# A two-layer hybrid transformer block on one core: the squares of the Strassen feed-forward moved to ScalarE, GpSimd's block sums held back, and the ends of that layer rearranged

## The chip, the core and the metric

The kernel runs on one core of a Trainium2 chip. Five engines work side by side and meet only through semaphores: TensorE (matmuls; PE in the profile), VectorE (DVE), ScalarE (ACT), GpSimd (POOL) and SyncE (SP), whose queue issues the loads. The metric is the device time of one execution in microseconds, lower is better.

## The reference, cut to what matters

```python
for layer in range(2):                       # x: 512 tokens, ctx: 256 tokens, width 1024
    ...                                      # norm, w_in, four mixers, w_out, x and ctx added to
    x = x + mod_l[5] * squared_relu_mlp(modulate(x, norm2_g[layer], mod_l[3], mod_l[4]),
                                        w_ff1[layer], w_ff2[layer])
    if need_ctx:                             # in layer 0 only
        ctx = ctx + ...                      # the same with mod_c
def squared_relu_mlp(h, w1, w2): return jnp.square(jax.nn.relu(h @ w1)) @ w2     # 1024 -> 4096 -> 1024
def rmsnorm(x, g): return x * lax.rsqrt(jnp.mean(x * x, -1) + EPS) * g
```

All of it is in float32. The kernel gets this precision from three passes per product: each operand is split into a rounded part ("hi", a copy on ScalarE) and what is left of it ("lo", a subtraction on VectorE or GpSimd), and TensorE adds up hi x hi, hi x lo and lo x hi.

## The kernel before

Activations lie transposed: `xT` holds 8 blocks of 128 features by T = 768 tokens (512 of x, 256 of ctx). No scheduler is involved. Each engine's program is written out by hand, and an engine works strictly in its written order; semaphores (`wait_ge`, `then_inc`) make it wait for the others. Weights come in units of 1 MB. `raw` has two slots, so SP issues the load of a unit as soon as the unit two places before it has been lowered (its lo part made) on GpSimd. The order of the units in layer 0's feed-forward is, for each chunk q: ff1 (q,0), ff1 (q,1), st (q,0), st (q,1).

**The feed-forward of layer 0** has 8 chunks (q = 0 to 7) of 512 hidden columns.

- ff1: two units j = 0, 1 of 256 columns. TensorE computes four groups each, (ct, s) = (0,0), (0,1), (1,0), (1,1): column half ct, and 512 (s = 0) or 256 (s = 1) tokens. The groups alternate between two PSUM banks (`gp`), and a bank is free again once ScalarE's `relu` has read it into `nsq`.
- The hidden values are squared (VectorE, in place) and turned into seven Strassen operands, in the order B11, T1, B21, T2, T3, T4, B22. T1 to T4 are sums (`h_sum`); each operand is copied by ScalarE (`h_high`) and subtracted by VectorE (`h_low`). A relu may overwrite `nsq` only when the operands that read it are lowered: that of (0,0) waits for T3's subtraction of the unit before.
- ff2: a Strassen product with 7 steps (`strassen`), in one unit per half of the output, st (q,0) and st (q,1); chunk 7 has only the first, and two ordinary units ff2 (7,2), ff2 (7,3) in place of the second. The weight blocks need four sums (`st_sum` n = 0 to 3) before they are copied (`block_high`, `fb_hi`, ScalarE) and subtracted (`fb_lo`, GpSimd, in `st_lower`). VectorE does these sums for st (q,0), GpSimd those for st (q,1). Sum n may be made only after GpSimd's subtraction n - 1; block copy 2 needs sum 1, copies 3 to 6 need sum 3.
- `st_add_back` on VectorE adds the steps' results to `xT`; step 2 needs the PSUM bank that step 0's add-back frees.

**The end of that layer.** `norm` of layer 1 needs the mean of squares: ScalarE squares the 8 blocks of `xT` (into `nsq`, two buffers), VectorE adds them up (`accumulate`, semaphore acc1), TensorE averages over the features, ScalarE takes logarithm and exponential, VectorE refines (L2225 to L2227) and scales (L2258), ScalarE makes `xhi` and VectorE `xlo`. The 256 ctx tokens go first, then the 512 of x; TensorE starts layer 1's first projection behind them. `after_unit` on ScalarE makes the hi part of the next weights.

## Time and profile before

| | us |
|---|---|
| median of 3 runs (2216.3 to 2225.04) | 2221.67 |
| the profiled execution | 2221.8 |
| its span | 2220.0 |
| busy in the span: TensorE, VectorE, ScalarE, GpSimd | 2027.1, 1226.8, 816.2, 806.2 |
| mean granted clock of TensorE | 0.958 |

The profile is one execution. Each row of a timeline has a start, the time it lasted, the engine, the line, what is written and read and how often; in brackets stands how long the engine had been idle and what it had waited for. A row with x4 is four instructions merged, its time that of all four. TensorE is the busiest engine by far, so the places where it stands still are the ones to read.

### The profile page before, as it was taken

The page shows a single profiled execution, that of the slowest core. Times are in us where ns is not written, and L with a number is a line of the kernel's source. Part 1 is how long each engine was busy: PE and PEld are TensorE (multiplying, and loading weights), DVE is VectorE, ACT ScalarE, POOL GpSimd, SP SyncE. Part 2 cuts the span into 40 slices and gives each one's busy share as a digit, 9 for nine tenths or more (in the row PEclk, how much of TensorE's full clock was granted, in tenths as well). Part 3 has the DMA queues.
Part 4 walks back from the last instruction along what each step waited for, and adds up shares of the span by engine and source line. Part 5 has one row for each costly group of instructions (what it writes and reads, how often), then busy time and mean ns, then how long its engine had stood idle before and what let it go on. Part 6 is the DMA issues. An engine that isn't in the chain of part 4 may idle for free.

```text
span 2220.0 us, 32559 instructions
## 1 busy us (share of the span) xinstructions
PE 2027.1 (91%) x13084; PEld 1720.0 (77%) x13084; DVE 1226.8 (55%) x2129; ACT 816.2 (37%) x1402; POOL 806.2 (36%) x641
## 2 busy tenths in 40 slices
PE   4899898989989799999999988998999888999998
PEld 3778786777877689889999867777787677778777
DVE  3555547846875666666666654545857765121122
ACT  2333324544454423333333333323554454232231
POOL 1231203012842255555565313213024523444452
PEclk8899998999999899999999999999999989999999
DMA  7320010452521121122211122010243312322322
GB/s 261 80 67 20 22 37 20 134 127 70 164 85 49 39 76 58 41 74 77 76 60 65 50 54 70 20 39 25 91 122 104 106 58 76 95 95 92 98 79 74
DMA packets 170694, 169.12 MB, mean 76 GB/s; under 512 B 29408, under 2 KB 159536, under 8 KB 170416
## 3 DMA queue, kind: packets, MB, share of 16 engines
q1 hardware_dynamic: 169744, 163.89, 24.2%
q10 hardware_dynamic: 800, 3.15, 0.4%
q8 instruction: 105, 1.72, 0.3%
q14 instruction: 45, 0.37, 0.1%
HBM read 159.15 MB, written 2.10 MB: 73 GB/s over the span
## 4 chain that ended last, share of the span: by engine, by line
PE 74%; DVE 13%; ACT 4%; issue 3%; DMA 2%; POOL 2%; SPq 2%; DVEq 0%; ACTq 0%; POOLq 0%
PE gp L1028 42%; PE sp L1287 3%; PE sp L1438 3%; PE gp L1324 2%; PE sp L1126 2%; PE gp L1082 2%; PE sp L1127 2%; PE sp L1128 2%; PE tp L1304 2%; SPq L833 1%; PE sp L1278 1%; PE gp L1052 1%; PE op L1304 1%; DVE small L2556 1%; DMA raw<-in_w_mod 1%
## 5 line engine op out<-in xcount | busy, mean ns | idle before, releaser
L917 POOL TENSOR_TENSOR wlo<-raw,whi 128x512 fp32r<-128x512 f32 x326 | 442.8, 1390 | 1029.4 <-ACT whi L1616 1029.2
L1028 PE MATMUL gp<-xhi,whi 128*128 128x512 f32 (+1 forms) x1416 | 517.4, 365 | 47.5 <-DVE xlo L2250 23.8
L1028 PE MATMUL gp<-xhi,wlo 128*128 128x512 f32 (+1 forms) x1416 | 503.8, 356 | 0.0
L1028 PE MATMUL gp<-xlo,whi 128*128 128x512 f32 (+1 forms) x1408 | 502.9, 357 | 0.0
L1028 PEld LDWEIGHTS gp<-xhi,whi 128*128 128x128 f32 x1416 | 275.4, 195 | 94.7 <-issue 23.2
L1028 PEld LDWEIGHTS gp<-xhi,wlo 128*128 128x128 f32 x1416 | 274.6, 194 | 39.3
L1028 PEld LDWEIGHTS gp<-xlo,whi 128*128 128x128 f32 x1408 | 273.7, 194 | 38.2 <-issue 1.8
L1616 ACT ACTIVATE whi<-raw 128x2048 fp32r<-128x2048 f32 (+2 forms) x86 | 159.0, 1849 | 205.1 <-PE gp L1028 129.5
L929 POOL TENSOR_TENSOR fb_lo<-raw,fb_hi 128x512 fp32r<-128x512 f32 x105 | 145.4, 1406 | 97.2 <-ACT fb_hi L1709 97.2
L2870 DVE SCALAR_TENSOR_TENSOR xT<-gp,mods,xT 128x512 f32<-128x512 f32 (+1 forms) x78 | 52.5, 680 | 172.2 <-PE gp L1028 160.3
L2556 DVE TENSOR_REDUCE small<-sp 128x1 f32<-128x768 f32 (+4 forms) x120 | 90.0, 792 | 51.3 <-PE sp L1287 51.3
L1028 PE MATMUL gp<-hhi,whi 128*128 128x512 f32 (+1 forms) x280 | 109.4, 391 | 3.5 <-issue 2.9
L1028 PE MATMUL gp<-hhi,wlo 128*128 128x512 f32 (+1 forms) x280 | 108.7, 388 | 0.0
L1028 PE MATMUL gp<-hlo,whi 128*128 128x512 f32 (+1 forms) x280 | 108.7, 388 | 0.0
L1709 ACT ACTIVATE fb_hi<-raw 128x512 fp32r<-128x512 f32 x105 | 59.6, 622 | 128.3 <-DVE raw L760 49.7
L2333 DVE SCALAR_TENSOR_TENSOR xT<-sp,mods,xT 128x128 f32<-128x128 f32 (+1 forms) x200 | 86.9, 490 | 33.0 <-PE sp L1128 32.7
L1126 PE MATMUL sp<-hhi,fb_hi 128*128 128x384 f32 x280 | 94.1, 336 | 6.3 <-DVE xT L2333 5.2
L2353 DVE TENSOR_TENSOR nsq<-nsq 128x512 f32<-128x512 f32 (+1 forms) x64 | 58.7, 920 | 65.5 <-ACT nsq L1686 65.3
L1127 PE MATMUL sp<-hlo,fb_hi 128*128 128x384 f32 x280 | 93.6, 334 | 0.0
L1128 PE MATMUL sp<-hhi,fb_lo 128*128 128x384 f32 x280 | 93.6, 334 | 0.0
L2302 DVE TENSOR_TENSOR hlo<-nsq,hhi 128x384 fp32r<-128x384 f32 (+1 forms) x112 | 77.5, 709 | 29.0 <-ACT hhi L1698 29.0
L1698 ACT ACTIVATE hhi<-nsq 128x384 fp32r<-128x384 f32 (+1 forms) x112 | 56.7, 528 | 92.4 <-DVE nsq L2317 53.4
(432 smaller groups left out, 4178.8 us busy)
## 6 DMA issues: line engine op xcount, KB each, us to landing
raw<-in_w_ff SPq DMA_DIRECT2D x63, 1024.0 KB, 5.4
raw<-in_w_mod SPq DMA_DIRECT2D x48, 1024.0 KB, 5.2
raw<-in_w_in SPq DMA_DIRECT2D x20, 1024.0 KB, 5.3
raw<-in_w_in SPq DMA_DIRECT2D x24, 256.0 KB, 4.6
bias<-e SPq DMA_DIRECT2D x96, 32.0 KB
raw<-in_w_out SPq DMA_DIRECT2D x12, 256.0 KB, 2.9
xin<-in_x ACTq DMA_DIRECT2D x1, 2048.0 KB, 9.7
raw<-in_w_out SPq DMA_DIRECT2D x16, 128.0 KB, 3.4
```

The source lines that it names most:

```text
L917: nc.gpsimd.tensor_tensor(wlo[:, s % 2, ks, :], raw[:, index[splits[s]] % 2, ks, :], whi[:, s % 2, ks, :].bitcast(F32), ALU.subtract)\
L929: nc.gpsimd.tensor_tensor(fb_lo[:, b, :, :, :], st_block(u, *ST_SOURCE[b]), fb_hi[:, b, :, :, :].bitcast(F32), ALU.subtract)\
L1028: mm = pe.matmul(out, lhs, rhs, start=(i == 0 and j == 0), stop=(i == end - 1 and j == 2))
L1126: pe.matmul(out, wh, high, start=(ST_OPENS[step] and m == 0), stop=False, skip_group_check=True)
L1127: pe.matmul(out, wh, low, start=False, stop=False, skip_group_check=True)
L1128: mm = pe.matmul(out, wl, high, start=False, stop=(m == 1), skip_group_check=True)
L1287: mm = pe.matmul(region(m, n, j, o, o + w), ql if i == 2 else qh, kl if i == 1 else kh, start=(i == 0 and not added), stop=(i == 2))
L1304: mm = pe.transpose((tp, op_)[half][:, P * (k - k0):P * (k - k0) + P], probs(m, n, j)[:, P * k:P * k + P], ident)
L1616: nc.scalar.activation(whi[:, s % 2, 0:k_tiles(v), :], raw[:, index[v] % 2, 0:k_tiles(v), :], ACT.Copy)\
L2302: V.tensor_tensor(low, src, high.bitcast(F32), ALU.subtract)\
L2333: ins = V.scalar_tensor_tensor(out=xT[:, k, a:b], in0=st_bank(u, step, pair)[:, a - lo:b - lo], scalar=mods[:, l, 40 + k, col:col + 1], in ...
L2556: V.tensor_reduce(small[:, c + j:c + j + 1], scored(m, n, j, w), AX.X, ALU.max, negate=True)\
```

## The change

Six edits, all around the feed-forward of layer 0 (lines by the diff):

1. The square of the hidden values is made by ScalarE right behind its relu, not by VectorE.
2. In chunk 0 the copies and sums of the first weight blocks come later: VectorE's sums 0 to 2 and ScalarE's block copies 0 to 2 behind the whole half j = 0, sum 3 and copies 3 to 6 into half j = 1.
3. In half j = 1 T4's sum moves behind the add-back of step 0.
4. GpSimd starts its sums for st (q,1) only when VectorE has added back step 0 of st (q,0).
5. For chunk 1 GpSimd lowers st (0,1) ahead of the weights of ff1 (1,0); ScalarE's copy of these weights moves behind the copies of st (0,1).
6. At the end, the last squares get two more buffers (`nsq2`, in the place of hidden blocks that are no longer read), `prepare` moves back, the weight copy moves behind the squares, and the two last add-backs and squares move into the first half of the normalisation.

```diff
+        nsq2, _ = place("nsq2", [P, 2, T], F32, scratch0 + 4 * T * 4)
+        last_square = lambda i: (nsq[:, 0, :], nsq[:, 1, :], nsq2[:, 0, :], nsq2[:, 1, :], nsq[:, 1, :], nsq2[:, 0, :])[i]
...
@@ st_lower (GpSimd)
+                if u[3]:
+                    pool.wait_ge(st_out, 2 * ST_STEPS * st_no["st", u[1], u[2], 0] + 2)
...
+                    if u in [("ff1", l, 1, 0) for l in ST_LAYERS]:
+                        st_lower(("st", u[1], 0, 1))
                     low(s)
...
-                    if j == 0 and q:
+                    if j == 0 and q > 1:
                         st_lower(("st", l, q - 1, 1))
@@ relu (ScalarE)
                 nc.scalar.activation(dst, bank(n)[:, 0:b - a], ACT.Relu).then_inc(bank_free[group_bank[n]], 1)
+                if l in ST_LAYERS:
+                    wait_read(act, None, n)
+                    nc.scalar.activation(dst, dst, ACT.Square).then_inc(ls(l, "h_sq"), 1)
@@ feed_forward_st (ScalarE)
-                            if j == 0 and (q == 0 or ct == 0):
-                                for b in range(3) if q == ct == 0 else range(3, ST_STEPS):
+                            if q == 0 and (j, ct) in ((0, 1), (1, 0)):
+                                for b in range(3) if j == 0 else range(3, ST_STEPS):
+                                    block_high(("st", l, 0, 0), b)
+                            if q and j == ct == 0:
+                                for b in range(3, ST_STEPS):
                                     block_high(("st", l, q, 0), b)
-                            if j == 1 and ct == (1 if q == 0 else 0):
+                            if q and j == 1 and ct == 0:
                                 after_unit(("ff1", l, q, 0))
...
-                    for i, k in enumerate((1, 3, 0, 2)):
...
                     u = ("ff2", l, ST_CHUNKS - 1, 2)
+                    for i, k in enumerate((1, 3, 0, 2, 4, 5)):
+                        if i < 4:
+                            act.wait_ge(st_out, 2 * ST_STEPS * st_no["st", l, ST_CHUNKS - 1, 0] + 11 + i)
+                        else:
+                            act.wait_ge(*upto(l + 1, "acc1", i - 3))
+                            for s in range(2):
+                                wait_read(act, None, N(u, (k % 2, s)))
+                        nc.scalar.activation(last_square(i), xT[:, k, :], ACT.Square).then_inc(ls(l + 1, "sq1"), 1)
                     after_unit(u)
-                    squares(l + 1, 1, 2, u)
                     u = ("ff2", l, ST_CHUNKS - 1, 3)
                     closing_squares(l + 1, 1, u, 0)
-                    norm(l + 1, 1, lambda: closing_squares(l + 1, 1, u, 1))
+                    norm(l + 1, 1, lambda: closing_squares(l + 1, 1, u, 1, done=True),
+                         {5: lambda: closing_square(l + 1, 1, u, 1, 0), 7: lambda: closing_square(l + 1, 1, u, 1, 1)})
@@ feed_forward_st (VectorE)
-                                a, b = SEGS[c[1]]
-                                wait_read(dve, None, N(u, c))
-                                V.tensor_tensor(nsq[:, ct, a:b], nsq[:, ct, a:b], nsq[:, ct, a:b], ALU.mult).then_inc(ls(l, "h_sq"), 1)
...
-                                if j == 0:
-                                    for n in range(3) if q == 0 else (3,):
-                                        st_sum(dve, V, first, n)
+                                if j == (0 if q else 1):
+                                    st_sum(dve, V, first, 3)
                                 continue
-                            for name in ("T2", "T3", "T4"):
-                                h_sum(l, q, j, name)
+                            h_sum(l, q, j, "T2")
+                            h_sum(l, q, j, "T3")
+                            if j == 0:
+                                h_sum(l, q, j, "T4")
...
                             st_add_back(first, 0)
+                            h_sum(l, q, j, "T4")
                             h_low(l, q, j, "T3")
...
-                    norm(l + 1, 1, closing=lambda: add_back(u, 5, l, cs=cs[2:]))
+                    prepare(l + 1)
+                    norm(l + 1, 1, inside={4: lambda: add_back(u, 5, l, cs=cs[2:3]), 6: lambda: add_back(u, 5, l, cs=cs[3:])})
```

ScalarE before, at the opening of chunk 0 (L1686 is the relu, L1698 an operand's copy, L1709 a block copy):

```order
L1686 ACTIVATE nsq<-gp 128x512 x2
L1698 ACTIVATE hhi<-nsq 128x384 x2
L1709 ACTIVATE fb_hi<-raw 128x512 x3
L1698 ACTIVATE hhi<-nsq 128x384 x5
L1709 ACTIVATE fb_hi<-raw 128x512 x4
L1686 ACTIVATE nsq<-gp 128x512
L1698 ACTIVATE hhi<-nsq 128x384
```

ScalarE now, at the same place (L1694 relu, L1697 the new square, L1709 an operand's copy, L1720 a block copy):

```order
L1694 ACTIVATE nsq<-gp 128x512
L1697 ACTIVATE nsq<-nsq 128x512
L1694 ACTIVATE nsq<-gp 128x512
L1697 ACTIVATE nsq<-nsq 128x512
L1709 ACTIVATE hhi<-nsq 128x384 x7
L1720 ACTIVATE fb_hi<-raw 128x512 x3
L1694 ACTIVATE nsq<-gp 128x512
L1697 ACTIVATE nsq<-nsq 128x512
L1709 ACTIVATE hhi<-nsq 128x384
```

All seven operands' copies of the half now stand together, with three block copies and not seven between the first two and the next relu.

VectorE before, in half j = 1, from the last square to the second add-back (L2353 square, L2317 an operand's sum, L2302 its subtraction, L2333 add-back):

```order
L2353 TENSOR_TENSOR nsq<-nsq 128x256
L2317 TENSOR_TENSOR nsq<-nsq 128x384 x3
L2302 TENSOR_TENSOR hlo<-nsq,hhi 128x384
L2333 SCALAR_TENSOR_TENSOR xT<-sp,mods,xT 128x384 x2
L2302 TENSOR_TENSOR hlo<-nsq,hhi 128x384
L2333 SCALAR_TENSOR_TENSOR xT<-tp,mods,xT 128x384
```

VectorE now, at the same place (L2340 sum, L2325 subtraction, L2356 add-back):

```order
L2340 TENSOR_TENSOR nsq<-nsq 128x384 x2
L2325 TENSOR_TENSOR hlo<-nsq,hhi 128x384
L2356 SCALAR_TENSOR_TENSOR xT<-sp,mods,xT 128x384 x2
L2340 TENSOR_TENSOR nsq<-nsq 128x384
L2325 TENSOR_TENSOR hlo<-nsq,hhi 128x384
L2356 SCALAR_TENSOR_TENSOR xT<-tp,mods,xT 128x384
```

The square is gone, and T4's sum stands behind the add-back of step 0.

ScalarE before, at the end of the layer (L1748, L1784, L1793 squares of `xT`, L1616 a weight copy, L1644 and L1645 logarithm and exponential, L1666 `xhi`):

```order
L1748 ACTIVATE nsq<-xT 128x768 x4
L1616 ACTIVATE whi<-raw 128x2048
L1784 ACTIVATE nsq<-xT 128x768 x2
L1793 ACTIVATE nsq<-xT 128x256 x2
L1644 ACTIVATE nrs<-sp,epsc 128x256
L1645 ACTIVATE nrs<-nrs 128x256
L1666 ACTIVATE xhi<-nt_85,mods 128x256 x8
L1793 ACTIVATE nsq<-xT 128x512 x2
```

ScalarE now (L1766, L1810 squares, nsq_77 being `nsq2`; L1622 weight copy; L1674 `xhi`):

```order
L1766 ACTIVATE nsq<-xT 128x768 x2
L1766 ACTIVATE nsq_77<-xT 128x768 x2
L1766 ACTIVATE nsq<-xT 128x768
L1766 ACTIVATE nsq_77<-xT 128x768
L1622 ACTIVATE whi<-raw 128x2048
L1810 ACTIVATE nsq<-xT 128x256 x2
L1650 ACTIVATE nrs<-sp,epsc 128x256
L1651 ACTIVATE nrs<-nrs 128x256
L1674 ACTIVATE xhi<-nt_86,mods 128x256 x5
L1810 ACTIVATE nsq<-xT 128x512
L1674 ACTIVATE xhi<-nt_86,mods 128x256 x2
L1810 ACTIVATE nsq<-xT 128x512
```

Six squares stand together in front of the weight copy, and the two of 512 columns stand among the eight `xhi` of the first half.

## Rows read from the trace of the kernel before

**Rows 1.** The page: the chain that ended last, by engine

```profile
PE 74%; DVE 13%; ACT 4%; issue 3%; DMA 2%; POOL 2%; SPq 2%; DVEq 0%; ACTq 0%; POOLq 0%
```

**Rows 2.** Waits of TensorE, 750 to 1300 us: engine, total, times, longest

```profile
PE gp L1028 <- ACT nsq L1686: 13.1, 2, 9.1
PE sp L1126 <- DVE xT L2333: 5.2, 5, 1.2
PE sp L1101 <- DVE nsq L2296: 3.3, 1, 3.3
PE gp L1028 <- DVE xlo L2250: 3.3, 1, 3.3
PE sp L1101 <- ACT nsq L1793: 3.1, 1, 3.1
PE tp L1126 <- DVE xT L2333: 2.3, 2, 1.2
PE sp L1126 <- POOL fb_lo L929: 1.1, 1, 1.1
```

**Rows 3.** Stretches: length, busy us of each engine, granted clock (PEclk), DMA

```profile
829.70:833.00 3.30, 3.23 (x9) 2.61 (x10) 2.63 (x4) 0.81 (x3) 0.88 (x1) 0.63 0.09 32
833.00:837.00 4.00, 4.00 (x17) 3.14 (x16) 1.36 (x3) 2.48 (x5) 1.25 (x1) 0.88 0.00 0
```

**Rows 4.** Timeline of TensorE: start, duration, instruction, idle before

```profile
829.77 0.51 PE L1028 MATMUL gp<-xhi,whi 128*128 128x512 f32 x1 [3.96 <-ACT nsq L1686]
...
862.21 0.41 PE L1126 MATMUL sp<-hhi,fb_hi 128*128 128x384 f32 x1 [1.12 <-DVE xT L2333]
...
895.69 0.39 PE L1028 MATMUL gp<-xhi,whi 128*128 128x512 f32 x1
```

**Rows 5.** Timeline of ScalarE at the opening of chunk 0

```profile
773.36 2.19 ACT L1709 ACTIVATE fb_hi<-raw 128x512 fp32r<-128x512 f32 x4 [1.54 <-DVE raw L764]
775.45 0.57 ACT L1686 ACTIVATE nsq<-gp 128x512 f32<-128x512 f32 x1
```

**Rows 6.** Timeline of VectorE at the opening of chunk 0

```profile
761.81 0.68 DVE L758 TENSOR_TENSOR raw<-raw 128x512 f32<-128x512 f32 x1
763.75 1.69 DVE L760 TENSOR_TENSOR raw<-raw 128x512 f32<-128x512 f32 x1 [1.25 <-POOL fb_lo L929]
...
769.24 1.61 DVE L2317 TENSOR_TENSOR nsq<-nsq 128x384 f32<-128x384 f32 x3
770.77 1.95 DVE L2302 TENSOR_TENSOR hlo<-nsq,hhi 128x384 fp32r<-128x384 f32 x4
```

**Rows 7.** Timeline of GpSimd in chunk 1 and at chunk 2's start

```profile
858.13 1.46 POOL L758 TENSOR_TENSOR raw<-raw 128x512 f32<-128x512 f32 x1
862.64 1.57 POOL L929 TENSOR_TENSOR fb_lo<-raw,fb_hi 128x512 fp32r<-128x512 f32 x1 [3.04 <-ACT fb_hi L1709]
...
885.08 5.50 POOL L917 TENSOR_TENSOR wlo<-raw,whi 128x512 fp32r<-128x512 f32 x4 [7.57 <-ACT whi L1616]
890.54 2.54 POOL L929 TENSOR_TENSOR fb_lo<-raw,fb_hi 128x512 fp32r<-128x512 f32 x2
```

**Rows 8.** Timeline of VectorE in chunk 1, half j = 1

```profile
858.48 2.59 DVE L2317 TENSOR_TENSOR nsq<-nsq 128x384 f32<-128x384 f32 x3
...
861.46 1.13 DVE L2333 SCALAR_TENSOR_TENSOR xT<-sp,mods,xT 128x384 f32<-128x384 f32 x2
```

**Rows 9.** Timeline of ScalarE at the first relu of chunk 2

```profile
894.26 0.58 ACT L1686 ACTIVATE nsq<-gp 128x512 f32<-128x512 f32 x1
```

**Rows 10.** Timeline of VectorE at the end of the layer

```profile
1271.50 0.96 DVE L2296 TENSOR_TENSOR nsq<-nsq 128x768 f32<-128x768 f32 x1 [0.99 <-ACT nsq L1784]
...
1291.07 0.70 DVE L2225 SCALAR_TENSOR_TENSOR sp<-sp,nrs 128x512 f32<-128x512 f32 x1 [4.24 <-ACT nrs L1645]
```

**Rows 11.** Timeline of ScalarE at the end of the layer

```profile
1266.42 1.92 ACT L1616 ACTIVATE whi<-raw 128x2048 fp32r<-128x2048 f32 x1 [1.93 <-PE gp L1028]
...
1286.20 1.29 ACT L1793 ACTIVATE nsq<-xT 128x512 f32<-128x512 f32 x2 [1.21 <-DVE xT L2870]
```

More of the change, by code:

```diff
@@ L1645, in rstd, with norm @@
                 nc.scalar.activation(nrs[:, a:b], nrs[:, a:b], ACT.Exp, scale=-0.5).then_inc(ls(l, f"rstd{which}"), 1)
-            def norm(l, which, between=None):
+            def norm(l, which, between=None, inside={}):
                 sh = 0 if which == 1 else 3
@@ L2229, in _, with norm @@
             averages = lambda i, end: sp_[:, 2 * i:2 * i + 2, :].rearrange("p b c -> p (b c)")[:, 0:end]
-            def norm(l, which, closing=None):
+            def norm(l, which, closing=None, inside={}):
                 if which == 1:
```

34 lines of the change are left out of this document (19 added, 15 removed).

## The prediction

> **What bounds the kernel now.** I read the chain of waits first: TensorE carries 74% of it [rows 1]. So an edit on another engine can only pay where TensorE stands still, and the second view was who TensorE waits for between 750 and 1300 us, the stretch that the diff touches (the layer-0 feed-forward of eight chunks, and the normalisation behind it). The list is short [rows 2]: 13.1 us in two waits for a relu on ScalarE (9.1 and 4.0), 7.5 us in seven waits for a Strassen add-back on VectorE (5.2 + 2.3, six of about 1.2 and one of 0.5), 1.1 us for a GpSimd subtraction, and 3.3 + 3.1 + 3.3 us in the closing normalisation. That is 31 us, and between these waits TensorE streams back to back. Nothing else in this stage can be won, and anything the change makes late enough appears as a new wait of the same kind.
>
> The third view was the clock of the stretch behind one wait. After the 3.96 us wait that ends at 829.77 [rows 4] the granted clock was 0.63 over 3.3 us and 0.88 over the next 4 us [rows 3], that is (0.37 x 3.3) + (0.12 x 4) = 1.7 us lost at the lower level of 1.2 GHz. A removed wait of that length takes this with it; the waits of 1.1 to 1.2 us show nothing of the sort.
>
> **The opening (first chunk).** TensorE stands 9.1 us because the relu that frees its bank runs only at 775.45 [rows 5]. In front of it on ScalarE are four block copies (from 773.36), and they wait for VectorE, which has to finish T2, T3, T4 and B22 of the first half, sums from 769.24 and subtractions from 770.77 [rows 6]. Ahead of those VectorE did, from 761.81 on, three block sums (the second took 1.69) and two squares, and only then B21's subtraction [rows 6]: of the 7.4 us up to 769.24, 1.1 are B21's copy and subtraction, 6.3 the rest. The rest leaves this place. In return ScalarE does two squares of 512 columns in front of the first copy, 0.64 each by the nearest row (two squares, 1.29, [rows 11]), but in the place of a square of 0.7 that VectorE did there. So the sums start about 6.3 - 0.4 = 5.9 us earlier, at 763.4. The last copy of the half ends near 765.9 (four copies behind the first sum, as the four from 773.36 take 2.19). Now come block copies 0 to 2 before the relu, and copy 2 needs VectorE's second block sum, which needs GpSimd's subtraction 0: 765.9 + 0.6 + 1.3 + 0.1, then 1.7 for the sum beside a busy GpSimd (763.75 in rows 6), then 0.6 for the copy: the relu starts at 770.2 instead of 775.45. **5.2 us**. The wait is still nearly 4 us long, so I leave its clock loss in. Bounds: 3.5 if ScalarE's squares are not covered, 6.5 if copy 2 is not held.
>
> **First to second chunk.** GpSimd now lowers the second Strassen unit of chunk 0 before the weights of the next ff1, so TensorE's wait for a subtraction goes (**1.1**). The larger part: before, the weights (1,0), then the unit, then the weights (1,1) came in this order, and the relu that TensorE waits 3.96 us for came behind the load of (1,1) and its subtractions. In the new order the unit's lows end about 11 us earlier (TensorE starts its unit 5 us earlier, GpSimd's 5.5 us of weights [885.08 in rows 7] are no longer in front), so the transfer of (1,1) starts that much earlier too. Following it (load, copy 1.9, four subtractions 5.5, subtraction 0, sum 1.7, copy 2, relu) gives a relu end 0.4 us after TensorE needs it: the wait falls from 3.96 to about 0.45, **3.5 us**, and with it the clock loss, **1.7 us**. What is queued behind the moved work: SP's loads for (1,1) and the next unit, both earlier; ScalarE's two weight copies now stand together and block it until the load lands, with only the block copies of the next unit behind them.
>
> **Steady chunks (1 to 6).** Each has one wait of 1.2 us: step 2 of the first Strassen unit needs the bank of step 0, and VectorE's add-back starts at 861.46 because the three sums T2 to T4, from 858.48, took 2.59 us [rows 8] while GpSimd ran the weights' last subtraction and its block sum (1.46, at 858.13) [rows 7]; the same three took 1.61 from 769.24, with GpSimd idle [rows 6]. The change takes T4's sum out of that place (1.61 / 3 = 0.54), keeps GpSimd quiet until the add-back (about 1.0), and turns the 256-column square, that VectorE did beside GpSimd, over to ScalarE. Together the add-back starts near 859.8 and TensorE needs it by 862.21 - 1.12 = 861.1 [rows 4]. The wait goes. What is late next? The relu of the next chunk's first group. It ends at 894.26 + 0.58 = 894.84 [rows 9] and TensorE takes the bank at 895.69 [rows 4]; with 0.1 for the signal it has 0.75 of slack. That relu stands at the end of a chain that GpSimd starts with its subtraction at 862.64 and that goes through a load, the weight subtractions and the pair from 890.54 [rows 7]. It is as long as before, so once TensorE gets there 1.2 sooner, all but the slack of 0.75 comes back as a wait. And GpSimd starts later: T4's copy can come only after T4's sum, now behind the add-backs (861.0 to 861.5), then B22's copy and block copy 0, so that its first subtraction is at 863.0, 0.36 later. Net gain of a chunk: 0.75 - 0.36 = 0.4, and six chunks **2.4 us**. Bounds: the chain is not delayed and shortens with the phase, 1.2 x 6 = 7.2; GpSimd's delay is 0.36 and a block sum, 1.46 [rows 7], 1.8 in all: 6 x (0.75 - 1.8), minus 6.3. Chunk 7 has no successor of the kind; its wait of 0.5 goes, **0.5**.
>
> A rule that speaks against the sum: the Trainium skill, "SBUF — State Buffer", section "Who interferes with whom", says that a VectorE instruction with two SBUF inputs and a GpSimd instruction that reads SBUF exclude each other, and that the one issued first holds the port for its whole length. The add-back that lets GpSimd go is the instruction in front of T4's sum, so both are issued together. By that rule, if GpSimd is first, T4's sum waits out a block sum; the price of that in this kernel's rows is the second rival below.
>
> **The end.** Before, TensorE waits for the fifth accumulation, which ends at 1271.50 + 0.96 = 1272.46 [rows 10]; squares and additions alternate, two buffers and one engine each, and the weight copy (1.92) stands in front of the last two squares at 1266.42 [rows 11]. With four buffers, only the last square depends on the last add-back, which ends near 1266.9: + 0.85 + 0.95 = 1268.8. TensorE itself arrives at 1269.1. Gain 3.4. From there to the second half of the normalisation, at 1291.07 [rows 10], took 18.6 us. New in it: the two add-backs move into the first sweep and the two squares (1.29 at 1286.20) beside it, -1.9; the weight copy, which lay beside TensorE's averages, now stands in front of the logarithm, +1.3; GpSimd's weight subtractions slide under the sweep and its port, +0.8. So 18.8. So the averages start 3.4 us earlier and the second half's normalisation 3.4 - 0.2, **3.2 us** (bounds 1.5 and 4.5). The position-bias loads behind this point are released by VectorE copies that follow the sweep and move with it.
>
> **Sum.** 5.2 + 1.1 + 3.5 + 1.7 + 2.4 + 0.5 + 3.2 = 17.6. The profiled execution took 2221.8 us (span 2220.0), and the median of the runs is 2221.7, so no correction is needed: 2221.8 - 17.6 = 2204.2 us.
>
> **Costs taken as nothing.** The squares on ScalarE in the rest of the chunks: each stands in the chain where VectorE's longer one stood, and the relu behind it has a bank to spare. The first pair of relus, 256 columns wide, grows by two squares inside the norm's sweep: 0.7 us that the sweep can be late at its second column block, against TensorE's own slower consumption of the blocks; uncovered it would cost those 0.7.
>
> **Rivals.**
> 1. The relocated wait does not come: GpSimd's chain rides along with the earlier phase, the steady chunks give 7.2 and not 2.4. For it: GpSimd, ScalarE and VectorE have idle time in every chunk. Against it: the load in the middle has a fixed length. 2204.2 - 7.2 + 2.4 = 2199.4 us.
> 2. GpSimd wins the port and its chain starts 1.8 later in each chunk. The steady chunks cost 6.3 where they gave 2.4: 2204.2 + 2.4 + 6.3 = 2212.9 us. For it: the 2.59 against 1.61. Against it: VectorE's next instruction is already queued, GpSimd has to notice a semaphore.
> 3. The two ends pay half: ScalarE's squares hold up the first relu (3.5 for 5.2), and the single weight copy before the logarithm eats the normalisation's gain (1.5 for 3.2). 2204.2 + 1.7 + 1.7 = 2207.6 us.
> 4. Slower: the held sums lose every alternation. If each of the four sum-and-subtraction pairs behind the hold waits for one VectorE instruction (1.0, what the three sums above grew by) on top of rival 2, the chain starts 1.8 + 4 x 1.0 = 5.8 later and TensorE waits 5.8 - 0.75 = 5.05 more in each of six chunks, 30.3 us: 2204.2 + 2.4 + 30.3 = 2236.9 us. It decides from a delay of 15.2 / 6 + 0.75 = 3.3 us per chunk, where the steady chunks eat the other 15.2 us. Against it: these pairs already alternated with VectorE before.
>
> **How the numbers follow.** Forecast 0.50, rival 1 0.17, rival 2 0.17, rival 3 0.12, rival 4 0.04. The likeliest case's own range is 2200 to 2208; with rivals 1 and 2 it is 2196 to 2214, which leaves out rival 4 and the far ends of the others. A measurement of this kernel tells 0.5%, 11 us, from no change: the limit is 2210.6. Forecast, rival 1, most of rival 3 and 0.35 of rival 2 lie below it: faster 0.81. The rest of 2 and 3: same 0.15. Slower 0.04.
>
> **What would show it.** In the profile after: the first relu wait near 4 us and not 9; no wait for a GpSimd subtraction in chunk 0; the wait at the second chunk's relu under 1 us and no low clock behind it; no wait of TensorE for step 2's bank in chunks 1 to 7, but one of 0.5 to 1 us for a relu at the first group of chunks 2 to 7 (absent: rival 1; near 2: rival 2); T4's sum at 0.56 (near 1.6: rival 2); TensorE at the averages without a wait for VectorE, and the second half's normalisation 3.2 us nearer to the end of the last Strassen step. I am wrong if a steady chunk does not get shorter, or if one of the two large waits at the opening stays.

## The result and the profile after

| | before | after |
|---|---|---|
| first measurement, median of 4 and 4 runs | 2223.36 | 2196.08 us, ratio 0.9893 [0.9868, 0.9918] |
| again, median of 17 and 6 runs | 2218.39 | 2203.56 us, ratio 0.9929 [0.9911, 0.9948] |
| first profiled execution | 2221.8 | 2205.76 us |

The ratios and their 95% intervals are the record's own estimates, not quotients of the two medians. The forecast was 2204.2 us, 0.9921 of the profiled 2221.8. The first median, 2196.08, lies below the likeliest range (2200 to 2208) and at the lower edge of the wider one (2196 to 2214), nearer to rival 1 (2199.4) than to the forecast; the second, 2203.56, lies on the forecast. So the total alone can't tell whether the sum was right, and the rest of the document goes by the traces.

The two intervals hardly meet, and much of the scatter arises outside the changed stage. The only matmul with 0.70 us put down to "issue" stands ahead of the stage, in code that no kernel of this study changes, and in the 14 profiles of this study it begins between 692.33 and 703.35 us. So I take it as zero. These are TensorE's landmarks before: zero, first Strassen matmul of chunk 1 (S1) and of chunk 7 (S7). The last landmark is layer 1's first matmul that reads `NA_y` (squares made by ScalarE), at 1310.07; it waits 1.8 us for them in every profile.

```profile
699.85 0.47 PE L1052 MATMUL gp<-xhi,whi 128*128 128x512 f32 x1 [0.70 <-issue]
...
856.73 0.34 PE L1126 MATMUL sp<-hhi,fb_hi 128*128 128x384 f32 x1
...
1242.43 0.34 PE L1126 MATMUL sp<-hhi,fb_hi 128*128 128x384 f32 x1
```

The same places after (start, duration, instruction, idle before it):

```profile
703.35 0.47 PE L1058 MATMUL gp<-xhi,whi 128*128 128x512 f32 x1 [0.70 <-issue]
...
849.09 0.34 PE L1132 MATMUL sp<-hhi,fb_hi 128*128 128x384 f32 x1
...
1231.08 0.34 PE L1132 MATMUL sp<-hhi,fb_hi 128*128 128x384 f32 x1
...
1295.45 0.27 PE L1191 MATMUL sp<-cf,NA_y 128*128 128x2 f32 x1 [1.81 <-ACT NA_y L1835]
```

From these rows the stage takes 610.22 us before and 592.10 after: 18.1 less, where 17.6 were forecast. The span fell by only 16.2, because the execution of after came to its zero 3.5 us later; 1.5 us more were gained behind `NA_y`. These 1.5 are TensorE's clock: over the first microseconds behind `NA_y` it was at 0.59 before and at 1.00 after (third number from the right), and the next group of such matmuls comes 8.58 us later before, 7.04 after. Before:

```profile
1312.00:1316.00 4.00, 4.00 (x12) 3.12 (x11) 0.00 (x0) 0.54 (x1) 3.38 (x3) 0.59 0.33 46
```

After:

```profile
1297.00:1301.00 4.00, 4.00 (x18) 3.24 (x18) 0.00 (x0) 0.93 (x1) 3.00 (x3) 1.00 0.30 43
```

All experiments are read by these landmarks (us behind zero; period is (S7 - S1) / 6):

| kernel | S1 | S7 | period | NA_y | ratio to before |
|---|---|---|---|---|---|
| before | 156.88 | 542.58 | 64.28 | 610.22 | |
| after | 145.74 | 527.73 | 63.67 | 592.10 | 0.9893 |
| after_again | 145.34 | 526.66 | 63.55 | 591.34 | 0.9929 |
| e1 without the hold | 145.33 | 530.12 | 64.13 | 594.96 | 0.9938 |
| e2 T4 in front | 145.19 | 523.32 | 63.02 | 588.36 | 0.9906 |
| e12 T4 in front, no hold | 145.23 | 527.06 | 63.64 | 591.96 | 0.9919 |
| e6 squares on VectorE | 146.33 | 533.07 | 64.46 | 598.14 | 0.9928 |
| e3 old end | 147.25 | 529.04 | 63.63 | 597.45 | 0.9938 |
| e4 old order at chunk 1 | 156.18 | 537.43 | 63.54 | 601.61 | 0.9963 |
| e5 old opening | 149.50 | 530.71 | 63.54 | 595.31 | 0.9929 |
| e11 before + new order | 148.86 | 534.60 | 64.29 | 605.43 | 0.9978 |
| e9 opening's relu first | 145.52 | 526.48 | 63.49 | 591.35 | 0.9903 |
| e8 weight copy behind the exponential | 145.49 | 525.90 | 63.40 | 591.43 | 0.9932 |
| e10 T4 in front, scales early | 145.06 | 523.38 | 63.05 | 588.17 | 0.9912 |

The ratios have intervals of about ±0.0015 to ±0.003 (3 to 7 us), wider than most single terms. Two profiles of the same kernel (after, after_again) differ by 0.4 at S1 and 0.8 at `NA_y`; what differs by less is not read. `NA_y` needs more care, for two reasons. The granted clock ahead of it and behind it differs from profile to profile: from there to the next group of such matmuls it is 8.6 us in before, e4 and e11, 10.2 in e6 and e9, and 7.0 in the others. And each kernel but after has one profile, so its scatter is not known; from `NA_y` to the end the 14 profiles take 903.8 to 911.5 us, in code that the edits don't touch. In after, e1, e3 and e6 one chunk is 1.0 to 1.7 us longer: ScalarE waits 10.1 to 11.0 us for the load of its weights there and 9.1 to 9.6 otherwise. Without it the period of after is 63.45.

The chain of waits of after, by engine (TensorE had 74%, GpSimd 2% [rows 1]):

```profile
PE 67%; DVE 13%; POOL 7%; ACT 5%; issue 3%; DMA 3%; SPq 2%; DVEq 0%; ACTq 0%; POOLq 0%
```

Its lines now name GpSimd's `fb_lo` with 3% and its `wlo` with 2%: the loop through GpSimd and the loads bounds part of the stage. TensorE's waits from 750 to 1300 (against [rows 2]):

```profile
PE gp L1034 <- ACT nsq L1694: 7.8, 8, 4.3
PE gp L1034 <- DVE xlo L2271: 5.4, 2, 5.0
PE sp L1191 <- ACT NA_y L1835: 1.8, 1, 1.8
PE sp L1107 <- ACT nsq L1810: 1.2, 1, 1.2
```

No wait for a Strassen add-back or a GpSimd subtraction is left. The eight waits for a relu are one of 4.28, six of 0.24 to 0.38 and one of 1.59 behind the late load; the second row is mostly the last wait of [rows 2], grown from 3.27 to 5.04. Stretches behind the waits that end at 774.93, 823.65 and 1280.17 (the granted clock again third from the right):

```profile
774.90:778.90 4.00, 3.97 (x9) 3.13 (x10) 2.02 (x4) 2.37 (x5) 0.85 (x1) 0.50 0.00 0
823.60:827.60 4.00, 3.95 (x17) 3.24 (x18) 2.00 (x4) 2.37 (x5) 0.87 (x1) 1.00 0.06 23
1280.10:1284.60 4.50, 4.43 (x11) 3.50 (x12) 4.39 (x7) 2.18 (x4) 0.00 (x0) 0.50 1.22 226
```

Where [rows 3] had 0.63, chunk 1's relu now waits 0.38 and the clock is full. Behind the opening's 4.28 us, and behind the 5.04, it is at the lower level, 0.50, that is 1.2 GHz.

The opening on ScalarE (before: [rows 5]): the third block copy waits for VectorE's sum, and the relu stands behind it, as the prediction said; 774.30 is 70.95 behind zero, before it was 75.60.

```profile
769.39 1.14 ACT L1720 ACTIVATE fb_hi<-raw 128x512 fp32r<-128x512 f32 x2
773.77 0.63 ACT L1720 ACTIVATE fb_hi<-raw 128x512 fp32r<-128x512 f32 x1 [3.23 <-DVE raw L761]
774.30 0.58 ACT L1694 ACTIVATE nsq<-gp 128x512 f32<-128x512 f32 x1
```

The middle of a steady chunk, number 3, on VectorE (before, in chunk 1: [rows 8]):

```profile
976.99 1.15 DVE L2340 TENSOR_TENSOR nsq<-nsq 128x384 f32<-128x384 f32 x2 [1.24 <-ACT nsq L1697]
978.14 0.56 DVE L2325 TENSOR_TENSOR hlo<-nsq,hhi 128x384 fp32r<-128x384 f32 x1
978.73 1.14 DVE L2356 SCALAR_TENSOR_TENSOR xT<-sp,mods,xT 128x384 f32<-128x384 f32 x2
979.79 0.55 DVE L2340 TENSOR_TENSOR nsq<-nsq 128x384 f32<-128x384 f32 x1
980.25 1.66 DVE L2325 TENSOR_TENSOR hlo<-nsq,hhi 128x384 fp32r<-128x384 f32 x1
```

Two sums take 1.15, the add-back starts 2.8 us behind the chunk's first Strassen matmul (before 4.7), and T4's sum takes 0.55. But the subtraction behind it takes 1.66 instead of 0.55: GpSimd, released by the add-back, started its sum at 979.95 (timeline of GpSimd):

```profile
979.95 1.55 POOL L759 TENSOR_TENSOR raw<-raw 128x512 f32<-128x512 f32 x1 [3.06 <-DVE xT L2356]
981.91 1.30 POOL L933 TENSOR_TENSOR fb_lo<-raw,fb_hi 128x512 fp32r<-128x512 f32 x1 [0.41 <-ACT fb_hi L1720]
```

The Trainium skill, "SBUF — State Buffer", section "Who interferes with whom", has the rule that I had weighed: the two engines exclude each other, and the first issued holds the port. By these rows T4's sum (0.55) was not held up, and the subtraction behind it, 1.66 beside GpSimd's 1.55, agrees with the rule.

### The profile page after: what moved, and what is told of

It reads as the page before. It is cut to its first block, busy times and chain, and to the rows that moved or that the text cites. A ratio compares the mean times of both kernels' runs of the same rounds, so it can differ in the third digit from the quotient of the medians.

```text
span 2203.8 us, 32564 instructions
## 1 busy us (share of the span) xinstructions
PE 2034.4 (92%) x13084; PEld 1726.0 (78%) x13084; DVE 1166.8 (53%) x2065; ACT 849.7 (39%) x1466; POOL 799.0 (36%) x641
## 4 chain that ended last, share of the span: by engine, by line
PE 67%; DVE 13%; POOL 7%; ACT 5%; issue 3%; DMA 3%; SPq 2%; DVEq 0%; ACTq 0%; POOLq 0%
PE gp L1034 41%; POOL fb_lo L933 3%; PE sp L1293 3%; PE sp L1444 3%; PE gp L1088 2%; DMA raw<-in_w_ff 2%; POOL wlo L919 2%; PE gp L1330 2%; PE tp L1310 2%; SPq L835 1%; DVE small L2580 1%; PE sp L1284 1%; PE gp L1058 1%; PE op L1330 1%; PE op L1310 1%
## 5 line engine op out<-in xcount | busy, mean ns | idle before, releaser
L1034 PEld LDWEIGHTS gp<-xhi,whi 128*128 128x128 f32 x1416 | 274.9, 194 | 89.3 <-issue 25.4
L1622 ACT ACTIVATE whi<-raw 128x2048 fp32r<-128x2048 f32 (+2 forms) x86 | 158.9, 1848 | 199.7 <-PE gp L1034 127.8
L933 POOL TENSOR_TENSOR fb_lo<-raw,fb_hi 128x512 fp32r<-128x512 f32 x105 | 138.1, 1336 | 77.8 <-ACT fb_hi L1720 77.8
L2325 DVE TENSOR_TENSOR hlo<-nsq,hhi 128x384 fp32r<-128x384 f32 (+1 forms) x112 | 76.6, 703 | 116.7 <-ACT hhi L1709 116.7
L1720 ACT ACTIVATE fb_hi<-raw 128x512 fp32r<-128x512 f32 x105 | 59.6, 621 | 120.9 <-DVE raw L761 48.7
L2356 DVE SCALAR_TENSOR_TENSOR xT<-sp,mods,xT 128x128 f32<-128x128 f32 (+1 forms) x200 | 86.8, 489 | 31.6 <-PE sp L1134 31.4
L2972 DVE TENSOR_TENSOR frel<-frel 128x512 f32<-128x512 f32 (+1 forms) x34 | 24.5, 721 | 105.9 <-ACT frel L1694 105.9
L1709 ACT ACTIVATE hhi<-nsq 128x384 fp32r<-128x384 f32 (+1 forms) x112 | 57.2, 529 | 44.5 <-DVE nsq L2340 42.4
```

The lines of the kernel that those rows point to most:

```text
L933: nc.gpsimd.tensor_tensor(fb_lo[:, b, :, :, :], st_block(u, *ST_SOURCE[b]), fb_hi[:, b, :, :, :].bitcast(F32), ALU.subtract)\
L1034: mm = pe.matmul(out, lhs, rhs, start=(i == 0 and j == 0), stop=(i == end - 1 and j == 2))
L1622: nc.scalar.activation(whi[:, s % 2, 0:k_tiles(v), :], raw[:, index[v] % 2, 0:k_tiles(v), :], ACT.Copy)\
L2325: V.tensor_tensor(low, src, high.bitcast(F32), ALU.subtract)\
L2356: ins = V.scalar_tensor_tensor(out=xT[:, k, a:b], in0=st_bank(u, step, pair)[:, a - lo:b - lo], scalar=mods[:, l, 40 + k, col:col + 1], in ...
```

## The experiments

**The order alone (e11).** The kernel before with `if u in [("ff1", l, 1, 0) ...]: st_lower(("st", u[1], 0, 1))` in front of `low(s)`, and the weight copy moved as in after.

```diff
-                    if j == 0 and q:
+                    if j == 0 and q > 1:
                         st_lower(("st", l, q - 1, 1))
...
-                            if j == 1 and ct == (1 if q == 0 else 0):
+                            if q and j == 1 and ct == 0:
                                 after_unit(("ff1", l, q, 0))
```

> The kernel before with one part of the change alone: at chunk 1 GpSimd lowers the second Strassen unit ahead of the weights (1,0), and ScalarE's weight copy moves behind that unit's copies. Theory A (GpSimd's chain bounds the first chunk, and the order takes 5.5 us of weights out of it): TensorE's 1.1 us wait for a GpSimd subtraction goes, the 3.96 us wait at chunk 1's relu falls under 0.6 with no slow clock behind it, the Strassen product of chunk 1 starts 150 to 151 us behind the landmark (before 156.9): 6 to 7 us faster than before, ratio 0.9970 to 0.9975. Theory B (it needs the new opening too): the wait at chunk 1's relu stays above 2 us and the gain is under 3 us.

The opening's wait stayed at 9.14, both waits behind it went, and S1 came 8.0 us earlier: theory A, and more than its 6 to 7. The ratio, 0.9978 [0.9963, 0.9993], is a smaller gain than its 0.9970 to 0.9975, and at `NA_y` only 4.8 of the 8.0 us are left. They were lost behind S7, where no edit of e11 reaches: behind the wait of 3.29 us for the accumulation the clock was at 0.50 in e11 and at 1.00 in before. GpSimd's weights (1,0), 5.37 us, stood in front of the unit in before; now they follow it (807.86), and the weights (1,1) begin at 815.61, 112.8 behind zero, where before they began at 120.2. GpSimd's timeline in e11:

```profile
807.86 5.03 POOL L917 TENSOR_TENSOR wlo<-raw,whi 128x512 fp32r<-128x512 f32 x4
815.61 2.54 POOL L917 TENSOR_TENSOR wlo<-raw,whi 128x512 fp32r<-128x512 f32 x2 [2.71 <-ACT whi L1618]
```

The same two in before:

```profile
791.65 5.37 POOL L917 TENSOR_TENSOR wlo<-raw,whi 128x512 fp32r<-128x512 f32 x4 [11.85 <-ACT whi L1616]
...
820.04 5.48 POOL L917 TENSOR_TENSOR wlo<-raw,whi 128x512 fp32r<-128x512 f32 x4 [7.58 <-ACT whi L1616]
```

**The old order in the changed kernel (e4).** The reverse of the edit above.

> The changed kernel with GpSimd and ScalarE in the old order at chunk 1 (weights (1,0), then the second Strassen unit of chunk 0, then weights (1,1)). Theory A (the order alone did it): TensorE's wait for a GpSimd subtraction in chunk 0 is back (about 1 us), and the wait for a relu at chunk 1's first unit is 3.5 to 4 us again with 1.7 us of low clock behind it; the stretch from TensorE's restart in chunk 0 to that point is 53.7 us and not 48.7; 5 to 6.3 us slower than the changed kernel, ratio 0.9915 to 0.9925. Theory B (the earlier opening pulled the chain along): the wait stays under 1.5 us, and the time is within 2 us of the changed kernel.

Theory A, and dearer than its 5 to 6.3 us (ratio 0.9963 where 0.9915 to 0.9925 were expected): the waits of 1.15 and 4.02 are back, with a granted clock of 0.58 behind the second and three smaller waits for GpSimd's subtractions (1.15 together) in front of them. S1 is at 156.18, only 0.7 better than before although TensorE restarted 3.4 us earlier. TensorE's timeline in e4:

```profile
803.96 0.44 PE L1130 MATMUL sp<-hhi,fb_hi 128*128 128x384 f32 x1 [1.15 <-POOL fb_lo L933]
...
825.01 0.50 PE L1032 MATMUL gp<-xhi,whi 128*128 128x512 f32 x1 [4.02 <-ACT nsq L1692]
```

GpSimd's weights (1,0) in e4:

```profile
787.09 5.47 POOL L919 TENSOR_TENSOR wlo<-raw,whi 128x512 fp32r<-128x512 f32 x4 [8.46 <-ACT whi L1620]
```

They begin 91.3 behind zero, before 91.8: they wait for their load and copy, and these do not follow TensorE's opening. SP issues the load when GpSimd has lowered st (0,0), which the new opening made later (82.9 behind zero, before 80.0), and the copy starts at 89.3 (before 89.8). The order is worth 10.6 us in the changed kernel (156.18 to about 145.5), 8.0 alone.

**The old opening (e5).** Block copies and sums of chunk 0 back among the operands.

```diff
-                            if q == 0 and (j, ct) in ((0, 1), (1, 0)):
-                                for b in range(3) if j == 0 else range(3, ST_STEPS):
...
+                            if j == 0 and (q == 0 or ct == 0):
+                                for b in range(3) if q == ct == 0 else range(3, ST_STEPS):
... (VectorE's sums likewise)
```

> The changed kernel with the block copies and block sums of chunk 0 in their old places (among the hidden values' operands). Theory A (their place is what held up the first relu): TensorE's wait there is 8.5 to 9.5 us and not 4.3, TensorE restarts 4.3 to 5 us later behind the landmark at 700 us than in the changed kernel (76 and not 71.6). Of this the next chunk keeps all if the terms of the sum were independent, as the prediction had them: chunk 1 starts 125 us behind the landmark (before 129.9, changed 120.3). Theory B (the squares on ScalarE did the larger part): wait under 6 us. Theory C (the two terms are one: the opening's gain is worth nothing without the new order, as the run with the old order showed, where chunk 1 started at 129.2 in spite of the early restart): chunk 1's start moves by less than 3 us.

Theory A for the wait (8.59, restart 75.87), and of its 4.3 us 3.8 remain at S1, so theory C is refuted: with the new order the opening pays. In the old order all of the change but the order (e4 against before) pays 0.7.

**The relu first (e9).** Block copies 0 to 2 behind the relu that TensorE waits for.

```diff
                                     relu(l, q, j, c)
+                                if q == 0 and (j, ct, i) == (1, 0, 0):
+                                    for b in range(3):
+                                        block_high(("st", l, 0, 0), b)
...
```

> The changed kernel with block copies 0 to 2 of chunk 0 behind the relu that TensorE waits for and not in front of it. Theory A: the relu then waits only for the operands of the half; the wait falls from 4.3 to under 1.5 us and its slow clock goes, TensorE restarts 3 to 4.3 us earlier (67.5 to 68.5 behind the landmark), and chunk 1 starts 2 to 5 us earlier (115.5 to 118.5). Theory B: GpSimd's chain for chunk 0 starts that much later, and the gain comes back as a wait for its subtractions or at chunk 1's relu: chunk 1 starts at 119.5 or later.

The wait of 4.28 is gone, and chunk 0's Strassen product starts 6.7 us earlier (75.48, after 82.21). Then TensorE waits twice for 2 us, and the product takes 36.3 us and not 29.1. TensorE's timeline in e9:

```profile
777.68 0.44 PE L1132 MATMUL tp<-hhi,fb_hi 128*128 128x384 f32 x1 [2.07 <-DVE hlo L2328]
...
781.01 0.66 PE L1132 MATMUL sp<-hhi,fb_hi 128*128 128x384 f32 x1 [2.01 <-DVE xT L2359]
```

S1 is where it was (145.52), as theory B said, but not by its path: TensorE does not wait for GpSimd, nor for chunk 1's relu, which starts 117.9 behind zero (after 119.7). It waits for VectorE, whose instructions now meet GpSimd's four subtractions: the two operand sums take 2.23 where they took 1.15. And behind the waits the clock is at 0.50 over 4 us and at 0.69 over the next 4. The waits are 4.1 us, and over the 3 and 4 us that TensorE worked there the clock cost (0.50 x 3) + (0.31 x 4) = 2.7: 6.8 of the 7.2 us by which the product is longer. So with 4.28 us of waiting taken away nothing was gained. VectorE in e9:

```profile
777.55 2.23 DVE L2343 TENSOR_TENSOR nsq<-nsq 128x384 f32<-128x384 f32 x2
```

GpSimd beside it:

```profile
773.44 5.33 POOL L933 TENSOR_TENSOR fb_lo<-raw,fb_hi 128x512 fp32r<-128x512 f32 x4 [3.58 <-ACT fb_hi L1720]
```

**The hold and T4's place (e1, e2, e12).** e1 drops the hold, e2 puts T4's sum in front of the add-back, e12 does both.

```diff
-                if u[3]:
-                    pool.wait_ge(st_out, 2 * ST_STEPS * st_no["st", u[1], u[2], 0] + 2)
...
-                            if j == 0:
-                                h_sum(l, q, j, "T4")
+                            h_sum(l, q, j, "T4")
...
                             st_add_back(first, 0)
-                            h_sum(l, q, j, "T4")
```

> The changed kernel without the hold of GpSimd's block sums. Theory A (the sum T4 moved away and the squares gone are enough): in the changed kernel the first add-back of chunk 1 ends near 852.5 us and TensorE needs it at the end of steps 0 and 1, 4.3 us after the Strassen step begins, near 853.4, so there is 0.9 us to spare. Without the hold the two sums T2 and T3 run beside GpSimd's block sum and grow from 1.15 to 1.7 to 2.0 us, which the 0.9 covers: no wait, or one under 0.2 us, of TensorE for VectorE in steady chunks; steady chunk period 63.4 us as with the hold; time within 2 us of the changed kernel (ratio to before 0.988 to 0.991). Theory B (the hold is what took the wait away): waits of 0.6 to 1.2 us for the add-back come back in six chunks, 4 to 7 us in all, ratio 0.991 to 0.993.

> The changed kernel with T4's sum in front of the add-back of step 0 again. Theory A: the add-back starts 0.55 us later, which the 0.9 us to spare covers, so no wait of TensorE for VectorE; T4's copy and so GpSimd's first subtraction come 0.3 to 0.5 us earlier, and the wait for the relu at the next chunk's first group (0.24 to 0.38 us) vanishes: the steady chunk period 63.1 instead of 63.4, 0 to 2 us faster than the changed kernel. Theory B (T4's place took the wait away): waits of 0.5 us or more for the add-back in steady chunks, period 63.9 or more, 3 us slower.

> The changed kernel with neither the hold nor T4's move: what is left in the steady chunks is the squares on ScalarE. Theory A (the hold matters because VectorE's operand sums, beside GpSimd, delay the add-back and everything behind it): the three sums take 2.4 to 2.6 us again, the add-back comes 0.6 to 1.1 us late against the 0.35 to spare with T4 in front, TensorE waits 0.3 to 0.8 us for it in each chunk, period 63.3 to 63.9 (63.0 with T4 in front and the hold, 63.45 changed, 63.9 without the hold, 64.3 before). Theory B (the squares' move alone is enough): no wait for the add-back, period 63.0 to 63.1.

e1 fell between the theories: no wait for the add-back (one of 0.16), as A said, but the period is 64.1 (64.0 without the late load), as slow as B. The two sums take 2.15 beside GpSimd, and the delay goes on into T4's copy, GpSimd's first subtraction (6.86 behind the chunk's first Strassen matmul, 5.98 in after) and the relu of the next chunk. VectorE in chunk 3 of e1 (the sums, a subtraction, the add-back):

```profile
972.66 2.15 DVE L2338 TENSOR_TENSOR nsq<-nsq 128x384 f32<-128x384 f32 x2 [1.25 <-ACT nsq L1695]
...
975.28 1.14 DVE L2354 SCALAR_TENSOR_TENSOR xT<-sp,mods,xT 128x384 f32<-128x384 f32 x2
```

e2 is theory A in full: three sums in 1.62, none of the relu waits but one of 0.18, period 63.0, and at `NA_y` 3.0 to 3.7 us earlier than after, more than its 0 to 2. A chunk of before without its wait is 64.28 - 1.16 = 63.1, so nothing is left to win there. GpSimd's first subtraction comes 0.19 us earlier than in after, its last of the unit 0.57, the next relu 0.69 (chunk 3). Only chunk 7 has a wait for the add-back again (0.52). VectorE at the same place in e2:

```profile
974.58 1.62 DVE L2340 TENSOR_TENSOR nsq<-nsq 128x384 f32<-128x384 f32 x3 [1.25 <-ACT nsq L1697]
976.12 0.55 DVE L2325 TENSOR_TENSOR hlo<-nsq,hhi 128x384 fp32r<-128x384 f32 x1
976.58 1.14 DVE L2356 SCALAR_TENSOR_TENSOR xT<-sp,mods,xT 128x384 f32<-128x384 f32 x2
977.64 0.55 DVE L2325 TENSOR_TENSOR hlo<-nsq,hhi 128x384 fp32r<-128x384 f32 x1
```

e12 is theory A too: three sums in 2.63, and in each chunk a wait for the add-back of 0.51 to 0.53 in place of 1.16. VectorE's three sums in chunk 3 of e12:

```profile
970.57 2.63 DVE L2338 TENSOR_TENSOR nsq<-nsq 128x384 f32<-128x384 f32 x3 [1.25 <-ACT nsq L1695]
```

And TensorE behind them:

```profile
974.34 0.41 PE L1130 MATMUL sp<-hhi,fb_hi 128*128 128x384 f32 x1 [0.52 <-DVE xT L2354]
```

So the squares on ScalarE bring 0.64 us a chunk (64.28 to 63.64), the hold another 0.62 with T4 in front (to 63.02), and T4's move takes 0.4 to 0.5 back.

**The squares back on VectorE (e6).**

```diff
-                if l in ST_LAYERS:
-                    wait_read(act, None, n)
-                    nc.scalar.activation(dst, dst, ACT.Square).then_inc(ls(l, "h_sq"), 1)
... (VectorE)
+                                V.tensor_tensor(nsq[:, ct, a:b], nsq[:, ct, a:b], nsq[:, ct, a:b], ALU.mult).then_inc(ls(l, "h_sq"), 1)
```

> The changed kernel with the hidden values' squares back on VectorE, in their old places, all else as changed. Theory A (the squares are a small part): the restart in chunk 0 is 0 to 1.5 us later (two squares of 512 and 256 columns in VectorE's queue ahead of the operands), waits of TensorE for the add-back in the steady chunks of 0 to 0.5 us (VectorE's second square runs beside GpSimd and delays the sums by 0.6 to 1.1, against 0.9 to spare), steady chunk period 63.3 to 63.7 (63.4 in the changed kernel): 0 to 3 us slower. Theory B (the squares carry the steady chunks): period 64.2, 5 us slower or more. The first wait of the stage (3.37 us at the landmark + 45.7) is 3.18 for xlo again, as before.

Theory B: period 64.46 (64.2 without one late load), `NA_y` 6 us late; the ratio, 0.9928, does not resolve it from after_again's. But the wait is one for the relu (0.54 to 1.05), not for the add-back: every delay of VectorE ahead of T4's copy comes out there. At S1 the squares matter by 0.6 to 1.0.

**The old end (e3).** Both engines' code behind the last chunk as before.

> The changed kernel with the end of the layer as before (squares with two buffers, weight copy in front of the last two, add-backs and squares between the halves of the normalisation). Theory A: the wait of 3.3 us of TensorE for the last accumulation is back, the averages start 14.7 us after the last Strassen step and not 11.3, and VectorE's normalisation of the second half starts 33.3 us behind that step and not 28.5; layer 1's first projections reach the bank that they wait for 2.9 to 4.8 us later: 3 to 5 us slower than the changed kernel, ratio 0.9905 to 0.9915. Theory B (the new end gives its gain back in its own wait of 5.0 us and the low clock behind it): the time is within 1.5 us of the changed kernel.

Theory A: from S7 to `NA_y` 68.4 us, against 64.4 and 64.7 in the two profiles of after (before 67.6). The wait of 3.29 is back, the one for `xlo` is 2.12 and not 5.04. Which part of edit 6 gives the gain was not run.

**The weight copy behind the exponential (e8).**

```diff
-                if n:
+                if n and not done:
                     after_unit(u)
                 rstd(l, which, n)
+                if n and done:
+                    after_unit(u)
```

> The changed kernel with the weight copy at the closing (1.9 us on ScalarE) behind the second half's logarithm and exponential and not in front of them. Theory A: it stands in the chain to TensorE's 5.0 us wait for xlo; that wait falls to 3.1 to 3.3 us, the slow clock behind it (matmuls of 0.43 us up to 1284.6) goes or shortens, and the next landmark, the matmul that waits for NA_y, comes 2 to 4 us earlier (588 to 590 behind the landmark, 592.1 in the changed kernel). Theory B: the copy is needed for the next weights (GpSimd's subtractions wait for it), and the gain comes back as a wait for GpSimd or at NA_y: under 1 us.

Neither: the wait grew to 5.74. VectorE's refinement did start 0.9 us nearer to S7, but GpSimd's weight subtractions, released by the copy, now ran beside the sweep's first instructions, two of which took 1.65 and 1.75 where 0.75 is usual. VectorE in e8:

```profile
1270.35 3.14 DVE L2283 SCALAR_TENSOR_TENSOR nt<-xT,amod,nrs 128x512 f32<-128x512 f32 x2
1273.42 1.75 DVE L2273 SCALAR_TENSOR_TENSOR xlo<-nt,mods,xhi 128x512 fp32r<-128x512 f32 x1
1275.20 1.65 DVE L2283 SCALAR_TENSOR_TENSOR nt<-xT,amod,nrs 128x512 f32<-128x512 f32 x1
```

GpSimd beside it:

```profile
1270.01 6.29 POOL L919 TENSOR_TENSOR wlo<-raw,whi 128x512 fp32r<-128x512 f32 x4 [12.51 <-ACT whi L1622]
```

**T4 in front, small operations early (e10), and the changed kernel again.** e10 is e2 with `prepare` and the scale factors (`amod`) moved in front of the add-backs `cs[2:]` of the unit ahead.

> The changed kernel with two edits: T4's sum in front of the add-back again, and the small VectorE operations in front of the closing normalisation (prepare and the scale factors, seven instructions of which three took 1.0 to 1.2 us each beside GpSimd's weight subtractions, 1258.32 to 1261.8) moved ahead of the last add-back of the unit before, where VectorE waits for TensorE. Theory A: the steady period is 63.0 us (TensorE never waits) as in the run with T4 in front; the normalisation starts when ScalarE's exponential ends, 0.8 us earlier; NA_y 587.5 behind the landmark (588.4 with T4 alone, 592.1 in the changed kernel); 3.5 to 5 us faster than the changed kernel in the median. Theory B: the small operations' gain is eaten by TensorE's wait at the second half, and NA_y stands at 588.4.

> The changed kernel itself, again, beside the others on one chip: median 2196 to 2202 us, ratio to before 0.988 to 0.992, and in the trace the landmarks of its first execution (restart in chunk 0 at 71.6 behind the landmark at 700, chunk 1 at 120.3, NA_y at 590.8 to 592.1, the lower one if the single wait of 1.6 us at one chunk does not come again).

after_again repeated the landmarks within 0.8 us; its median (2203.56) and ratio (0.9929) missed the 2196 to 2202 and 0.988 to 0.992 expected. e10 has 2196.81 on the same chip; the intervals 0.9912 [0.9891, 0.9933] and 0.9929 [0.9911, 0.9948] overlap, so the total does not prove it, but `NA_y` is 3.2 to 3.9 us earlier, within 0.2 us all of it T4's place (e2: 588.36). The small operations took 0.2 instead of 1.0 to 1.2 us each, and brought nothing at `NA_y`: theory B.

## Why the prediction was right, and where not

**The opening and the second chunk (forecast 5.2 + 1.1 + 3.5 + 1.7 = 11.5).** At S1 it is 11.1 and 11.5. The relu moved 4.65 us and not 5.2: the restart is 76.23 to 71.58 behind zero. The operand sums came 5.8 us earlier for the forecast 5.9 (the squares' net cost was put at 0.4 where the rows named give 0.6); then the first block sum, beside GpSimd's first subtraction, took 1.76 us and not the 0.68 of [rows 6], which the prediction had not counted:

```profile
770.31 1.76 DVE L759 TENSOR_TENSOR raw<-raw 128x512 f32<-128x512 f32 x1
```

The waits went as said (none for GpSimd; 0.38 for the forecast 0.45; full clock). But the split was wrong, and with it the idea of independent terms: the order alone gives 8.0 (e11) where 1.1 + 3.5 + 1.7 = 6.3 were booked, and everything but the order 0.7 (e4 against before); on top of the order the opening gives 3.1 to 4.2 (e11 and e5 against the two profiles of after). The step that failed is the one that booked TensorE's earlier restart as gain by itself. In the old order GpSimd's weights, unit and next weights decide when chunk 1 can go on (e4), and the new opening does not make them earlier; in the new order VectorE's operands and the clock took back what e9 gained at the restart. That the sum of the four terms fits within 0.4 us is therefore in part luck. (The opening was not run alone: e4 has the squares, the hold and T4's place too, and e11 lacks them.)

**Steady chunks (forecast 2.4).** Measured over six chunks 385.70 - 381.99 = 3.7, and 4.4 in after_again. The mechanism held: the wait for step 2's bank vanished and one of 0.2 to 0.6 for the next chunk's relu took its place (0.5 to 1 were forecast). In chunk 3 that relu starts 37.5 us behind the chunk's first Strassen matmul before and after: the chain kept its length. So rival 1 (no relocated wait) is refuted, and rival 2 and 4 with it, since GpSimd's first subtraction comes 0.07 us later behind the chunk's first Strassen matmul (5.91 before, 5.98 after), not 0.36 or 1.8. But the chain can be shortened: without T4's move it is 0.7 us shorter, almost no relu is waited for, and e2 gains 7.6 us over the six chunks, which rival 1 had priced at 7.2. Two things were mis-stated. T4's move was booked among what removes the wait. It is not needed (e2: three sums end in time), and by delaying T4's copy and by VectorE's and GpSimd's work meeting behind it, it costs 0.4 to 0.5 us a chunk, about 3 in all; what it does remove is chunk 7's wait of 0.5. And the squares' move, which got no figure of its own, is half of what can be gained (e12: 0.64 of 1.26 a chunk).

**Chunk 7 and the end (forecast 0.5 + 3.2 = 3.7).** From S7 to `NA_y` 67.64 before, 64.37 and 64.68 after: 3.0 to 3.3. The averages start 26.3 us behind S7 and not 30.1 (0.5 + 3.4 = 3.9 forecast), without a wait for VectorE, and the second half's normalisation 43.5 and not 48.6, 5.1 nearer where 3.7 were forecast: the stretch between the two, put at 18.8, took 17.2. ScalarE in after, the weight copy and the logarithm behind it (before: [rows 11]):

```profile
1271.42 1.90 ACT L1622 ACTIVATE whi<-raw 128x2048 fp32r<-128x2048 f32 x1
1273.22 0.67 ACT L1650 ACTIVATE nrs<-sp,epsc 128x512 f32<-128x512 f32 x1
```

VectorE's second half in after (before: [rows 10]):

```profile
1274.59 0.70 DVE L2246 SCALAR_TENSOR_TENSOR sp<-sp,nrs 128x512 f32<-128x512 f32 x1 [2.56 <-ACT nrs L1651]
...
1276.78 2.57 DVE L2281 SCALAR_TENSOR_TENSOR nt<-xT,amod,nrs 128x512 f32<-128x512 f32 x2
```

TensorE restarts 5.6 us behind this point, and did before (1291.07 to 1296.60). But its wait grew from 3.27 to 5.04 us [rows 2], and behind it the clock was at 0.50 for 4.5 us; behind before's 3.27 it was at 1.00. From the restart to `NA_y` it is 15.3 to 15.6 us after and 13.5 before. This loss of 1.8 to 2.1 was in no term, and it is what 5.1 shrank to 3.0 to 3.3 by. Of the three profiles with the old end before's is the fastest: from S7 to `NA_y` it is 68.4 in e3 and 70.8 in e11, where the clock behind the wait of 3.29 was at 0.62 and 0.50 and not at 1.00. So what the new end is worth depends on the clock that the old one gets: 3 us by the one profile of before, over 6 by e11. Rival 3 (the two ends pay half) is not borne out: the relu moved 4.65 and not 3.5, chunk 7 and the end gave at least 3.0 and not 0.5 + 1.5.

**Cost taken as nothing.** The squares of the first two narrow relus did show: the stage's first wait is 3.37 us for a relu where it was 3.18 for `xlo`, 0.15 to 0.3 us later behind zero and not the 0.7 at risk.

The sum was right to 0.5 to 1.3 us at `NA_y` (18.1 and 18.9 for 17.6) because its errors (opening and end too high, order and steady chunks too low) cancel. That is luck. And at the next group of such matmuls, past before's low clock, the gain is 19.7 and 20.4.

## What to carry to other kernels

When two edits serve the same chain, run each alone and both: the order alone gave 8.0 us, all but the order 0.7, together 11.3. The longest wait of the bounding engine may be worth nothing if the next wait closes behind it (in e9 for VectorE's operands, slowed by GpSimd); find that place first. And read a change of 1% by landmarks inside the trace, from the last point ahead of the stage, since this kernel's start of the stage alone scatters by 11 us; and look at the granted clock behind every landmark before a difference is read.
